# Norms and last output blocks by halves of the tokens in a two-layer hybrid encoder

## The chip, the cores and the metric

The kernel runs as one launch on one core of a Trainium2 chip. The time is device microseconds (us) of that core: the median of three runs was 3239.95 (3239.34 to 3239.95). The engines are named as in the profile: PE is TensorE, PEld its weight load, DVE is VectorE, ACT is ScalarE, POOL is GpSimd, SP is SyncE, which issues most DMAs.

## The reference

Two layers over 1024 tokens of width 1024 (float32). Cut to what matters:

```
h = x; c_act = silu(c)
for i in 0, 1:
    sh_m, sc_m, g_m, sh_f, sc_f, g_f = split(c_act @ ada_w[i] + ada_b[i])    # modulation
    hn = rms_norm(h, norm_mix[i]) * (1 + sc_m) + sh_m
    y = dsa_mixer(hn) if i == 0 else rwkv7_mixer(hn)
    h = h + g_m * y
    hn = rms_norm(h, norm_ffn[i]) * (1 + sc_f) + sh_f
    u = causal depthwise conv of width 3 over tokens (hn @ w_up[i]) + conv_b[i]
    h = h + g_f * ((silu(u[:, :2816]) * u[:, 2816:]) @ w_down[i])
return rms_norm(h, norm_final)
rms_norm(x, g) = x / sqrt(mean(x * x over the width) + 1e-6) * g
```

The first mixer scores all keys for each token with a small indexer, keeps the top 256 admissible ones, and runs 16 heads of latent attention on them. The second is an RWKV-7 recurrence. Both end in a projection by a 1024 x 1024 matrix.

## The kernel before, in words

Activations lie with the width on the 128 partitions: h is 8 tiles (KT) of 128 x 1024 tokens (S). A half (HALF) is 512 tokens, and each matmul writes 128 x 512. Every large product is made of three passes of matmuls, high by high, high by low and low by high (`passes3`, L137). The high and low parts of weights are made by POOL: SP loads a block of 128 output columns to one of two staging buffers `w_raw`, POOL writes `w_hi` by a multiplication with ones (L149) and `w_lo` by a subtraction (L151), two operations each for half a block. `stream_loop` (L155) does this for a stage. A load waits until the block two earlier is split, the split waits until the block two earlier is used.

Each engine has one instruction stream, the order of the code's parts (`k.parts`). The streams meet by semaphores, and a stage ends in a barrier of PE, ACT and DVE (`stage_end`, L125). No scheduler reorders them.

The joints between stages are all alike. An output block m of a projection or of the FFN's down product is added to h by DVE over all 1024 tokens (L767, L864, L1684: "residual"). `NormFront` (L423) then has ACT square that tile (L444) and DVE add it up (L453). After the last block, PE sums the accumulated squares over the partitions by 8 matmuls with one column (`pe_end`, L467). Then comes `norm_stage` (L472): mean on DVE (L517), root on ACT with the load of its table (L500), reciprocal on DVE (L524), 8 transposes on PE that spread it (L512), and for each tile a scaled tile (DVE, L545), its high part (ACT, L505) and its low part (DVE, L531). PE takes a tile when its low part is there.

The FFN has 22 tiles of width in 11 parts of two; the down product adds 8 output blocks of two tiles each (12 matmuls) into h in every part. Ten parts go through a loop and one, the last, follows it. Modulation vectors of later stages are made beside: DVE multiplies rows of `ada_w` by c (L620, L1676), PE sums over the partitions (L627, L1646).

In the attention, DVE searches the threshold of the top 256 keys by bits, one block of 128 queries per search: rounds (`look`, `settle`) and at the end of each search `search_end`. Nineteen rounds (`EARLY`, L1490) of the first search stand ahead of the loop over pairs of heads, the rest and other searches inside it. After the loop ACT issues loads of h (L1379, h had been spilled) and of six modulation rows (L1629), and then makes the high parts of the attention's output (`split_tiles`, L828), DVE the low parts (L833); the projection's PE waits for each.

`out_stage` (L2970) is the last: the norm without modulation writes y (L545), PE transposes it (64, L2989), ACT and DVE copy rows of 128 tokens, SP stores them.

## Time and profile before

| | us |
|---|---|
| median of three runs | 3239.95 |
| profiled execution | 3243.58 |
| its span | 3241.8 |
| PE busy in it | 2996.2 (92%) |
| DVE busy | 1661.1 (51%) |
| POOL busy | 1472.4 (45%) |
| ACT busy | 1077.8 (33%) |
| mean granted clock of TensorE | 0.957 |

The profile is of one execution, and its rows are of that one. The span runs from its first to its last instruction. Busy shares are means over stages that differ. What a joint costs is read from the timeline: the last matmul ahead of it, the first behind it, and what each of PE's waits was for. Numbers in square brackets of a row are the idle time before it and the instruction that ended it. A granted clock of 1.0 is 2.4 GHz, of 0.5 it is 1.2 GHz. Grouped rows (x8) give the time over the whole group. A matmul of float32 ones with one column has two records (16 for 8).

### The profile page before, as it was taken

What the parts mean: (1) busy time and instruction counts of PE and PEld (TensorE: products, weight loads), DVE (VectorE), ACT (ScalarE), POOL (GpSimd) and SP (SyncE); (2) the same over time, 40 slices, a digit from 0 to 9 for tenths busy, and PEclk for the clock granted to TensorE, in tenths of its full rate; (3) what the DMA queues carried; (4) which work ended last, traced back from release to release, by engine and by line L of the source; (5) the groups of instructions that cost most, each with busy time, mean ns of one, the idle gap of its engine ahead of it and who ended that gap; (6) DMA issues with size and microseconds to landing.
All of it is one profiled execution on the core that took longest, in us unless ns stands there. A gap on an engine that the chain in (4) does not pass through costs nothing.

```text
span 3241.8 us, 62740 instructions
## 1 busy us (share of the span) xinstructions
PE 2996.2 (92%) x25842; PEld 2379.9 (73%) x25842; DVE 1661.1 (51%) x2291; ACT 1077.8 (33%) x1634; POOL 1472.4 (45%) x1464
## 2 busy tenths in 40 slices
PE   5889899889999999998999798999898999999997
PEld 5734467777878877786678588888777888778886
DVE  4477887665444544457033255665545444443446
ACT  2267787222111211125332255455312211211112
POOL 1101000335666656666365355565364554555543
PEclk6889999999999999998999799999998999999998
DMA  5300000522322222221532311211211111111112
GB/s 204 119 12 14 1 2 2 204 82 74 90 83 66 73 74 84 84 59 51 191 121 80 111 49 50 89 56 51 86 49 39 46 41 42 44 55 52 40 42 73
DMA packets 229752, 225.80 MB, mean 70 GB/s; under 512 B 16398, under 2 KB 198241, under 8 KB 229537
## 3 DMA queue, kind: packets, MB, share of 16 engines
q1 hardware_dynamic: 217232, 180.42, 18.0%
q10 hardware_dynamic: 12305, 42.25, 3.6%
q8 instruction: 167, 2.74, 0.4%
q14 instruction: 48, 0.39, 0.0%
HBM read 185.15 MB, written 37.22 MB: 69 GB/s over the span
## 4 chain that ended last, share of the span: by engine, by line
PE 43%; issue 19%; POOL 18%; DVE 8%; DMA 5%; ACT 3%; POOLq 1%; SPq 0%; DVEq 0%; ACTq 0%; PEldq 0%; PEld 0%
POOL w_hi L149 9%; POOL w_lo L151 9%; PE ps L139 7%; PE ps L141 7%; PE ps L140 7%; DMA w_raw<-in_f_w_up_dram 2%; PE ps L2571 2%; DMA w_raw<-in_f_w_down_dram 2%; PE ps L2583 2%; PE ps L1187 2%; PE ps L1176 1%; PE ps L1198 1%; PE ps L2496 1%; PE ps L2620 1%; PE ps L2610 1%
## 5 line engine op out<-in xcount | busy, mean ns | idle before, releaser
L149 POOL TENSOR_TENSOR w_hi<-w_raw,ones 128x128 fp32r<-128x128 f32 (+1 forms) x568 | 471.6, 830 | 1074.1 <-PE ps L141 950.1
L751 DVE SCALAR_TENSOR_TENSOR uc<-u,pc,uc 128x1024 f32<-128x1024 f32 x176 | 272.0, 1546 | 602.2 <-ACT uc L735 589.2
L139 PE MATMUL ps<-hn_hi,w_hi 128*128 128x512 f32 x1408 | 553.2, 393 | 26.6 <-POOL w_lo L151 18.5
L151 POOL TENSOR_TENSOR w_lo<-w_raw,w_hi 128x128 fp32r<-128x128 f32 (+1 forms) x568 | 554.3, 976 | 44.5
L140 PE MATMUL ps<-hn_lo,w_hi 128*128 128x512 f32 x1408 | 550.2, 391 | 0.0
L141 PE MATMUL ps<-hn_hi,w_lo 128*128 128x512 f32 x1408 | 550.1, 391 | 0.0
L734 ACT ACTIVATE u<-ps 128x1024 f32<-128x1024 f32 x88 | 90.5, 1028 | 939.1 <-PE ps L141 934.4
L139 PEld LDWEIGHTS ps<-hn_hi,w_hi 128*128 128x128 f32 x1408 | 265.8, 189 | 90.4 <-issue 18.1
L141 PEld LDWEIGHTS ps<-hn_hi,w_lo 128*128 128x128 f32 x1408 | 265.6, 189 | 55.8
L140 PEld LDWEIGHTS ps<-hn_lo,w_hi 128*128 128x128 f32 x1408 | 265.9, 189 | 54.8
L139 PE MATMUL ps<-g_hi,w_hi 128*128 128x512 f32 x704 | 279.8, 397 | 10.7 <-POOL w_lo L151 9.7
L767 DVE SCALAR_TENSOR_TENSOR h<-ps,mod,h 128x1024 f32<-128x1024 f32 x176 | 220.4, 1281 | 123.6 <-PE ps L141 123.6
L141 PE MATMUL ps<-g_hi,w_lo 128*128 128x512 f32 x704 | 274.5, 390 | 0.0
L140 PE MATMUL ps<-g_lo,w_hi 128*128 128x512 f32 x704 | 274.4, 390 | 0.0
L139 PE MATMUL ps<-rp_x_hi,w_hi 128*128 128x512 f32 x448 | 180.6, 403 | 4.4 <-DVE rp_x_lo L531 4.4
L141 PE MATMUL ps<-rp_x_hi,w_lo 128*128 128x512 f32 x448 | 177.8, 397 | 0.0
L140 PE MATMUL ps<-rp_x_lo,w_hi 128*128 128x512 f32 x448 | 177.3, 396 | 0.0
L139 PEld LDWEIGHTS ps<-g_hi,w_hi 128*128 128x128 f32 x704 | 132.1, 188 | 61.4 <-issue 23.6
L141 PEld LDWEIGHTS ps<-g_hi,w_lo 128*128 128x128 f32 x704 | 132.1, 188 | 28.1
L140 PEld LDWEIGHTS ps<-g_lo,w_hi 128*128 128x128 f32 x704 | 132.2, 188 | 25.5
L1856 DVE SCALAR_TENSOR_TENSOR rp_x<-rp_hn,pc,rp_x 128x1024 f32<-128x1024 f32 x24 | 41.8, 1750 | 159.7 <-ACT rp_x L1831 159.7
L1807 POOL TENSOR_TENSOR w_hi<-w_raw,ones 128x512 fp32r<-128x512 f32 x48 | 59.9, 1248 | 136.1 <-PE ps L141 125.9
(380 smaller groups left out, 5652.1 us busy)
## 6 DMA issues: line engine op xcount, KB each, us to landing
w_raw<-in_f_w_up_dram SPq DMA_DIRECT2D x88, 512.0 KB, 3.9
f_ada_w<-in_ada_w_dram SPq DMA_DIRECT2D x48, 512.0 KB, 3.9
rwkv_scratch<-rp_stage ACTq DMA_DIRECT2D x48, 512.0 KB, 3.0
w_raw<-in_f_w_down_dram SPq DMA_DIRECT2D x176, 128.0 KB, 2.2
rc_raw<-rwkv_scratch SPq DMA_DIRECT2D x32, 512.0 KB, 4.0
d_r<-in_ada_w_dram ACTq DMA_DIRECT2D x24, 512.0 KB, 5.8
ada_w<-in_ada_w_dram SPq DMA_DIRECT2D x16, 512.0 KB, 8.6
xin<-in_x_dram SPq DMA_DIRECT2D x8, 512.0 KB, 7.2
```

Of the source, the lines that this page charges most:

```text
L139: pe.matmul(out, w_hi, x_hi, start=first, stop=False)
L140: pe.matmul(out, w_hi, x_lo, start=False, stop=False)
L141: return pe.matmul(out, w_lo, x_hi, start=False, stop=last)
L149: pool.tensor_tensor(hi, raw, one, ALU.mult).then_inc(k.w_hi_done, 1)
L151: pool.tensor_tensor(k.w_lo[s][:, tiles, :], raw, hi.bitcast(F32), ALU.subtract).then_inc(k.w_split if n else k.w_half, 1)
L734: act.activation(u[wi][:, 2:S + 2], k.ps[2 * s + wi][:, :], ACT.Copy).then_inc(f["u_copy"], 1)
L751: dve.scalar_tensor_tensor(out=c[wi][:, :], in0=u[wi][:, tap:tap + S], scalar=k.pc[:, bass.ds(i * (2 * FF_TILES) + col, 1)], in1=c[wi][:, ...
L767: dve.scalar_tensor_tensor(out=k.h[:, m, :], in0=k.ps[m % (3 if last else 4)][:, :], scalar=k.mod[:, gate:gate + 1], in1=k.h[:, m, :], op0 ...
L1187: last = pe.transpose(turn(c)[:, i * P:(i + 1) * P], x[A % 2][e][:, t * P:(t + 1) * P], k.ident[:, :])
L1807: pool.tensor_tensor(hi, raw, one, ALU.mult).then_inc(k.w_hi_done, 1)
L2571: last = pe.matmul(bank(4 + h)[hs(1 - c), at(x)], tg[hs(c), x, h, G_M, :], ul[hs(c), 0, h, x, :], start=True, stop=True)
L2583: u_last = pe.matmul(bank(h)[hs(c), at(x)], ul[hs(1 - c), 1, h, x, :], z[hs(1 - c), h, x, :], start=begin, stop=lv == LV[-1], skip_group_c ...
```

## The change

- **Norms by halves.** Squares, sums, mean, root, reciprocal and transposes are made for 512 tokens at a time, and each tile in two halves: 16 scaled, high and low parts of 128 x 512. The first half's numbers are made while PE still works on the second half's output blocks. The second half's last squares, its mean, reciprocal and transposes stand inside the next stage, between the half tiles. PE's first product of the next stage takes all tiles of the first half, then those of the second.
- **Projections.** The last two output blocks (6 and 7) are made half by half: (6,0), (7,0), (6,1), (7,1), with the first half's sums and transposes set in (6,1) and (7,1).
- **FFN.** The last part's 8 blocks come from two loads of 512 KB (128x2x512). POOL splits them by four pairs of 512-wide operations into what was `hn_lo`. PE waits for both and does 16 steps of 6 matmuls, the 8 blocks of half 0 first, and adds each step's half tile to h by DVE.
- **Output.** `out_stage` is gone. ACT writes h times the gain to y beside the last steps, PE transposes it unscaled by the root, rows 0 to 3 during steps 11 to 14, and the reciprocal root is a scale of the copy out of PSUM. Eight row buffers take the place of four.
- **Attention.** 22 rounds ahead of the loop, the ends of the searches 2 to 5 set earlier and, for 4 and 5, in parts. At its end the high and low parts come ahead of the loads of h and of the rows, and ahead of DVE's run of semaphore clears.
- `dynamic_dma_scratch_size` is 4096 in the program's build.

The diff, cut to its core:

```diff
+def stream_last(k, sources, his, los):
+    b0, landed0, hi0 = k.blocks, list(k.landed), k.hi_extra
+    def raw(s):
+        return k.w_raw[s][:, :, :].rearrange("p a b -> p (a b)")
+    def sp_part(sp):
+        for j, source in enumerate(sources):
+            sp.wait_ge(k.w_split, b0 + j + 1)
+            sp.dma_start(raw(j).rearrange("p (t n) -> p t n", n=HALF), source).then_inc(k.w_landed[j], 16)
+    def pool_part(pool):
+        for j in range(2):
+            pool.wait_ge(k.w_landed[j], landed0[j] + 16)
+            pool.wait_ge(k.w_used, b0)
+            for n in range(2):
+                cols = slice(n * HALF, (n + 1) * HALF)
+                pool.tensor_tensor(his[j][:, cols], raw(j)[:, cols], k.ones[:, 0:1].to_broadcast([P, HALF]), ALU.mult
+                                   ).then_inc(k.w_hi_done, 1)
+                pool.wait_ge(k.w_hi_done, (b0 + j) * 2 + (hi0 + n + 1))
+                pool.tensor_tensor(los[j][:, cols], raw(j)[:, cols], his[j][:, cols].bitcast(F32), ALU.subtract
+                                   ).then_inc(k.w_split if n else k.w_half, 1)
+    k.parts["sp"].append(sp_part)
+    k.parts["pool"].append(pool_part)
+    k.blocks += 2
...
+    def ms_dve(self, dve, h):
+        nm, at = self.k.nm, self.part(h)
+        dve.wait_ge(nm["sum"], self.summed(h))
+        dve.tensor_scalar(self.ms[:, at], self.sums[:, at], 1.0 / D, EPS, ALU.mult, ALU.add).then_inc(nm["ms"], 1)
+    def root_act(self, act, h):
+        nm, at = self.k.nm, self.part(h)
+        if h == 0:
+            act.activation(self.k.root0[:, :], self.k.ones[:, 0:1], ACT.Sqrt)
+        act.wait_ge(nm["ms"], 2 * self.n + h + 1)
+        act.activation(self.root[:, at], self.ms[:, at], ACT.Sqrt).then_inc(nm["root"], 1)
+    def rinv_dve(self, dve, h):
+        nm, at = self.k.nm, self.part(h)
+        dve.wait_ge(nm["root"], 2 * self.n + h + 1)
+        dve.reciprocal(self.rinv[:, at], self.root[:, at]).then_inc(nm["rinv"], 1)
+    def bcast_pe(self, pe, h):
+        nm = self.k.nm
+        pe.wait_ge(nm["rinv"], 2 * self.n + h + 1)
+        for tt in range(h * TT // 2, (h + 1) * TT // 2):
+            last = pe.transpose(self.bcast[:, tt * P:(tt + 1) * P], self.rinv[:, tt:tt + 1].to_broadcast([P, P]),
+                                self.k.ident[:, :])
+        last.then_inc(nm["bcast"], 1)
+class FirstFront(NormStats):
...
+    def sums_pe(self, pe, h):
+        k, nm = self.k, self.k.nm
+        last_of = max(i for i, (_, n) in enumerate(self.order) if n == h)
+        pe.wait_ge(nm["acc"], self.acc0 + self.added(last_of + 1))
+        for tt in range(h * TT // 2, (h + 1) * TT // 2):
+            last = pe.matmul(self.sums[:, tt:tt + 1], k.sq_acc[:, tt * P:(tt + 1) * P], k.ones[:, 0:1], start=True, stop=True)
+        last.then_inc(nm["sum"], 4)
+TAIL = ((KT - 2, 0), (KT - 1, 0), (KT - 2, 1), (KT - 1, 1))
+BLOCKS_ORDER = tuple((m, n) for m in range(KT - 2) for n in range(NH)) + TAIL
+HALVES_ORDER = tuple((m, n) for n in range(NH) for m in range(KT))
...
+        if not rest:
+            for h in range(2):
+                front.ms_dve(dve, h)
+            front.scale_dve(dve)
+            for h in range(2):
+                front.rinv_dve(dve, h)
+        scaled(0)
+        if between:
+            between(dve)
+        scaled(1)
+        for i in range(LAST):
+            low(i)
+            if rest and i == 2:
+                for j in range(LAST - rest, LAST):
+                    front.dve(dve, j)
+            if rest and i == 4:
+                front.ms_dve(dve, 1)
+            if rest and i == 6:
+                front.rinv_dve(dve, 1)
+            if i + 2 < LAST:
+                scaled(i + 2)
 
     def pe_part(pe):
...
+def second_half(front):
+    def norm_pe(pe, i):
+        if i == 3:
+            front.sums_pe(pe, 1)
+        if i == 6:
+            front.bcast_pe(pe, 1)
+    return norm_pe
...
-    b2 = stream_loop(k, None, [(lambda i, m=m: down_block(PARTS // 2, 0, m), FF_TILES) for m in range(KT)])
+    b2 = stream_last(k, [w_down[:, FT - FF_TILES:FT, j * HALF:(j + 1) * HALF] for j in range(2)],
+                     [hn_lo[:, j, :] for j in range(2)], [hn_lo[:, 2 + j, :] for j in range(2)])
...
+    def last_bank(q):
+        return k.ps[q % 4 // 2][:, q % 2 * HALF:(q % 2 + 1) * HALF]
+    def pe_last(pe):
+        pe.wait_ge(f["g_free"], tiles0 + FT + 1)
+        for j in range(2):
+            pe.wait_ge(k.w_split, b2 + j + 3)
+        for q, (m, n) in enumerate(HALVES_ORDER):
+            cols = slice(n * HALF, (n + 1) * HALF)
+            pe.wait_ge(f["resid"], end0 + (q // 2 + 1 if q < 4 else q + 1))
+            for kt in range(FF_TILES):
+                w = slice(kt * HALF + m % 4 * P, kt * HALF + (m % 4 + 1) * P)
+                last = passes3(pe, last_bank(q), hn_lo[:, m // 4, w], hn_lo[:, 2 + m // 4, w],
+                               g_hi[:, kt, cols], g_lo[:, kt, cols], kt == 0, kt == FF_TILES - 1)
+                if q == 0 and kt == 0:
+                    last.then_inc(k.w_used, 2)
+            last.then_inc(f["last"], 1)
+            if layer == 0 and q == 3:
+                pe_mod(pe, 5)
+            if q == 10:
+                front.sums_pe(pe, 0)
+            if layer == 0 and q == 12:
+                front.bcast_pe(pe, 0)
+            if layer and 11 <= q < 15:
+                turned(pe, q - 11, range(KT))
...
+    def pe_out(pe):
+        pe.wait_ge(f["resid"], end0 + 4 + LAST)
+        for tt in (4, 5):
+            turned(pe, tt, range(KT - 1))
+        front.sums_pe(pe, 1)
+        for tt in (4, 5):
+            turned(pe, tt, (KT - 1,))
+        for tt in (6, 7):
+            turned(pe, tt, range(KT))
...
+    def out_act(act, tt, cols=slice(0, S)):
+        act.wait_ge(o_t, tt + 1)
+        act.wait_ge(k.nm["rinv"], 2 * front.n + tt // 4 + 1)
+        act.activation(row_of(tt)[:, cols], k.ps[(2, 2, 2, 2, 2, 0, 1, 2)[tt]][:, cols], ACT.Copy,
+                       scale=front.rinv[:, tt:tt + 1]).then_inc(copied[0], 1)
...
+def tail_dve(k, dve, front, b0, gate_col, resid, tail, ready=None, between=None):
+    for i, (m, n) in enumerate(TAIL):
+        cols = slice(n * HALF, (n + 1) * HALF)
+        if n:
+            block_done(k, dve, b0 + m)
+        else:
+            dve.wait_ge(tail, i + 1)
+            if ready:
+                ready(dve, m)
+        gate = gate_col + m
+        dve.scalar_tensor_tensor(out=k.h[:, m, cols], in0=k.ps[m % 3][:, cols], scalar=k.mod[:, gate:gate + 1],
+                                 in1=k.h[:, m, cols], op0=ALU.mult, op1=ALU.add).then_inc(resid, 1)
+        if i < 3:
+            front.dve(dve, 2 * (KT - 2) + i)
+        if i == 1:
+            if between:
+                between(dve)
+            front.ms_dve(dve, 0)
+            front.rinv_dve(dve, 0)
...
-        act.wait_ge(sem["pv"], NP)
-        for m in range(KT):
-            act.dma_start(k.h[:, m, :], spill[m, :, :]).then_inc(h_back[m], 16)
...
-    EARLY = 19
+    EARLY = 22
...
-        return {13: (2,), 14: (3,), 15: (4,), 16: (5,)}.get(A, ())
+        return {10: (2,), 11: (3,)}.get(A, ())
...
-            for m, ranked in ((6, LAST - 3), (7, LAST + 6)):
-                if A == (LAST - 4 if m == 6 else LAST + 6):
+            for m, begun, ranked in ((4, 12, 13), (5, 14, 15), (6, LAST - 4, LAST - 3), (7, LAST + 6, LAST + 6)):
+                if A == begun:
                     end_above(dve, m)
                 if A == ranked:
                     end_rank(dve, m)
-                if A == ranked + 1:
+                if A == ranked + (1 if m > 5 else 0):
...
+    x_ready = split_tiles(k, "d_o", x, x_hi, x_lo)
+    k.parts["act"].append(back_act)
     k.parts["act"].append(act_first)
-    x_ready = split_tiles(k, "d_o", x, x_hi, x_lo)
     k.parts["act"].append(act_rest)
+    k.parts["dve"].append(clear_dve)
```

Three places show how the streams are changed. ACT at the attention's end, before; d_r in the DMA row are the modulation rows' buffers, d_o_hi is the high part of the attention's output:

```order
L1318 ACTIVATE d_r,d_small<-d_r,d_small 128x1024 x2
L1303 ACTIVATE d_r<-ps 128x512 x4
L1311 ACTIVATE d_lat<-ps 128x512
L1379 DMA h<-dsa_h 128x1024 x8
L1629 DMA d_r<-in_ada_w_dram 128x1024 x6
L828 ACTIVATE d_o_hi<-d_o_t 128x1024 x8
```

and after:

```order
L1622 ACTIVATE d_r,d_small<-d_r,d_small 128x1024 x2
L1607 ACTIVATE d_r<-ps 128x512 x4
L1615 ACTIVATE d_lat<-ps 128x512
L1075 ACTIVATE d_o_hi<-d_o_t 128x1024 x8
L1907 DMA h<-dsa_h 128x1024 x8
L1935 DMA d_r<-in_ada_w_dram 128x1024 x6
```

The eight high parts have moved ahead of the 14 DMA issues.

DVE at the joint before the first FFN, before: L1684 is the residual, L453 the sum of squares, L545 the scaled tile, L531 the low part:

```order
L1684 SCALAR_TENSOR_TENSOR h<-ps,mod,h 128x1024
L453 TENSOR_TENSOR d_lat<-d_lat 128x1024
L1692 TENSOR_TENSOR mod<-ps,pc 128x24
L517 TENSOR_SCALAR nm_small<-ps 128x8
L520 TENSOR_SCALAR scl<-mod 128x8
L522 TENSOR_TENSOR scl<-scl,pc 128x8
L524 RECIPROCAL nm_small<-nm_small 128x8
L545 SCALAR_TENSOR_TENSOR nm_t_0<-h,scl,ps 128x1024
L545 SCALAR_TENSOR_TENSOR nm_t_1<-h,scl,ps 128x1024
L531 SCALAR_TENSOR_TENSOR hn_lo<-nm_t_0,mod,hn_hi 128x1024
```

and after, from the fourth low part on: L633 is the scaled half tile, L639 the low part, L487 the mean and L499 the reciprocal of the second half:

```order
L639 SCALAR_TENSOR_TENSOR hn_lo<-nm_t_0,mod,hn_hi 128x512
L487 TENSOR_SCALAR nm_small<-ps 128x4
L633 SCALAR_TENSOR_TENSOR nm_t_1<-h,scl,ps 128x512
L639 SCALAR_TENSOR_TENSOR hn_lo<-nm_t_0,mod,hn_hi 128x512
L633 SCALAR_TENSOR_TENSOR nm_t_1<-h,scl,ps 128x512
L639 SCALAR_TENSOR_TENSOR hn_lo<-nm_t_1,mod,hn_hi 128x512
L499 RECIPROCAL nm_small<-nm_small 128x4
L633 SCALAR_TENSOR_TENSOR nm_t_0<-h,scl,ps 128x512
L639 SCALAR_TENSOR_TENSOR hn_lo<-nm_t_1,mod,hn_hi 128x512
```

The L633 behind the reciprocal is half tile 8, the first of the second half; the L639 behind it is the low part of half tile 7. The second half's numbers stand between the first half's tiles.

PE at the program's end, before, from the last three of 96 matmuls of the last part on: L467 are the sums of squares, L512 the transposes of the root, L2989 those of the output:

```order
L139 MATMUL ps<-g_hi,w_hi 128x512
L140 MATMUL ps<-g_lo,w_hi 128x512
L141 MATMUL ps<-g_hi,w_lo 128x512
L467 MATMUL ps<-ones,sg 128x1 x8
L512 MATMUL ps<-ident,nm_small 128x128 x8
L2989 MATMUL ps<-ident,y 128x128 x64
```

and after, the last step's six matmuls (hn_lo holds the weights' parts) and what stands about them:

```order
L875 MATMUL ps<-ident,y 128x128 x8
L143 MATMUL ps<-g_hi,hn_lo 128x512
L144 MATMUL ps<-g_lo,hn_lo 128x512
L145 MATMUL ps<-g_hi,hn_lo 128x512
L143 MATMUL ps<-g_hi,hn_lo 128x512
L144 MATMUL ps<-g_lo,hn_lo 128x512
L145 MATMUL ps<-g_hi,hn_lo 128x512
L875 MATMUL ps<-ident,y 128x128 x14
L573 MATMUL ps<-ones,sq_acc 128x1 x4
L875 MATMUL ps<-ident,y 128x128 x18
```

Transposes of the output (L875) now stand ahead of the last step, and the last sums (L573) among them; L512's are gone here.

## Rows read from the trace of the kernel before

**Rows 1.** The page's busy time, share and instructions of each engine:
```profile
PE 2996.2 (92%) x25842; PEld 2379.9 (73%) x25842; DVE 1661.1 (51%) x2291; ACT 1077.8 (33%) x1634; POOL 1472.4 (45%) x1464
```

**Rows 2.** PE's waits: line, releaser, total us, times, longest us:
```profile
PE ps L512 <- DVE nm_small L524: 15.2, 5, 5.0
PE ps L139 <- DVE hn_lo L531: 8.1, 2, 4.1
```

**Rows 3.** Timeline, projection to FFN: start, us, instruction [idle before <-releaser]:
```profile
686.29 1.84 PE L1646 MATMUL ps<-ones,d_r 128*128 128x1 f32 x16
690.18 3.01 PE L467 MATMUL ps<-ones,d_lat 128*128 128x1 f32 x16 [2.05 <-DVE d_lat L453]
695.43 1.94 PE L512 MATMUL ps<-ident,nm_small 128*128 128x128 f32 x8 [2.24 <-DVE nm_small L524]
697.41 2.47 DVE L545 SCALAR_TENSOR_TENSOR nm_t<-h,scl,ps 128x1024 f32<-128x1024 f32 x2 [2.12 <-PE ps L512]
701.44 0.77 PE L139 MATMUL ps<-hn_hi,w_hi 128*128 128x512 f32 x1 [4.07 <-DVE hn_lo L531]
```

**Rows 4.** Windows: busy us by engine, granted clock, DMA share, GB/s:
```profile
357.00:360.00 3.00, 2.75 (x16) 1.36 (x14) 2.93 (x11) 2.46 (x8) 0.00 (x0) 0.54 0.01 3
701.00:704.00 3.00, 2.56 (x6) 2.10 (x7) 2.93 (x4) 1.21 (x2) 0.00 (x0) 0.50 0.94 290
```

**Rows 5.** Timeline of PE, second projection to FFN:
```profile
2447.24 0.39 PE L141 MATMUL ps<-rc_y_hi,w_lo 128*128 128x512 f32 x1
...
2447.92 0.39 PE L141 MATMUL ps<-rc_y_hi,w_lo 128*128 128x512 f32 x1
...
2463.82 0.76 PE L139 MATMUL ps<-hn_hi,w_hi 128*128 128x512 f32 x1 [4.07 <-DVE hn_lo L531]
```

**Rows 6.** Timeline, attention output to its projection:
```profile
580.88 3.78 ACTq L1379 DMA_DIRECT2D h<-dsa_h  x8
...
588.20 7.69 ACT L828 ACTIVATE d_o_hi<-d_o_t 128x1024 fp32r<-128x1024 f32 x8 [8.46 <-issue]
...
591.22 0.77 PE L139 MATMUL ps<-d_o_hi,w_hi 128*128 128x512 f32 x1 [10.38 <-DVE d_o_lo L833]
```

**Rows 7.** Timeline of PE in the attention loop:
```profile
356.31 1.65 PE L1176 MATMUL ps<-d_k_t,d_o_t 64*128 64x384 f32 x4 [3.27 <-DVE d_small L1563]
```

**Rows 8.** Timeline of PE, setup to attention:
```profile
83.05 0.80 PE L139 MATMUL ps<-d_hn_hi,w_hi 128*128 128x512 f32 x1 [3.87 <-DVE d_hn_lo L531]
```

**Rows 9.** Timeline, end of the first FFN and next stage's start:
```profile
1435.59 0.46 POOL L151 TENSOR_TENSOR w_lo<-w_raw,w_hi 128x128 fp32r<-128x128 f32 x1
...
1439.60 1.28 DVE L767 SCALAR_TENSOR_TENSOR h<-ps,mod,h 128x1024 f32<-128x1024 f32 x1 [1.44 <-PE ps L141]
1440.81 5.48 DVE L620 SCALAR_TENSOR_TENSOR f_ada_acc<-f_ada_w,cact,f_ada_acc 128x1024 f32<-128x1024 f32 x4
...
1481.79 0.77 PE L139 MATMUL ps<-rp_x_hi,w_hi 128*128 128x512 f32 x1 [4.38 <-DVE rp_x_lo L531]
```

**Rows 10.** The page's DMA issues: count, KB each, median us to landing:
```profile
w_raw<-in_f_w_up_dram SPq DMA_DIRECT2D x88, 512.0 KB, 3.9
```

**Rows 11.** Timeline of POOL, 512-wide splits behind the second projection:
```profile
2448.46 1.04 POOL L149 TENSOR_TENSOR w_hi<-w_raw,ones 128x512 fp32r<-128x512 f32 x1 [5.08 <-PE ps L141]
2449.58 1.27 POOL L151 TENSOR_TENSOR w_lo<-w_raw,w_hi 128x512 fp32r<-128x512 f32 x1
2450.80 2.08 POOL L149 TENSOR_TENSOR w_hi<-w_raw,ones 128x512 fp32r<-128x512 f32 x1
```

**Rows 12.** Timeline, second FFN's end and the output stage:
```profile
3181.29 0.46 POOL L151 TENSOR_TENSOR w_lo<-w_raw,w_hi 128x128 fp32r<-128x128 f32 x1
...
3206.63 0.39 PE L141 MATMUL ps<-g_hi,w_lo 128*128 128x512 f32 x1
...
3218.65 10.62 DVE L545 SCALAR_TENSOR_TENSOR y<-h,pc,ps 128x512 f32<-128x512 f32 x16 [2.12 <-PE ps L512]
```

**Rows 13.** Timeline of VectorE, scoring before the attention loop:
```profile
200.18 5.03 DVE L1527 SCALAR_TENSOR_TENSOR d_dist<-d_r,d_wi,d_dist 128x512 f32<-128x512 f32 x6 [0.31 <-ACT d_r L1334]
```

532 lines of the change are left out of this document (310 added, 222 removed).

## The prediction

> **What bounds the kernel now.** I read the page's busy row first: TensorE (PE) is busy for 2996.2 of 3241.8 us [rows 1]. A change that leaves its matmuls alone can only win in the 245 us in which it waits, and in what a wait costs behind it. The waits of PE come next [rows 2]: five waits for the reciprocal of the norm's root take 15.2 us, two for the first low part of the normalised tile 8.1. They stand at a few joints between stages, so I went through these one by one in the timeline.
>
> The joint before the first FFN shows the pattern [rows 3]. The last output matmul ends near 686.45; PE's queue then issues, from 686.29, 16 sums for modulation, then 2.05 us idle, 16 sums of squares, 2.24 idle, 8 transposes that spread the reciprocal root, 4.07 idle, and the first FFN matmul at 701.44: 15.0 us, of which 6.8 is PE work. Then PE runs at half its clock: granted 0.50 from 701 to 704 (1.2 GHz of 2.4), behind an idle stretch of 4 us [rows 4]. The joint before the second FFN is the same, 2448.15 to 2463.82, 15.67 us; its rows also give PE's pace at full clock, three matmuls in 0.68 us, 0.227 each [rows 5].
>
> All sums below are made against the profiled execution (3243.58 us, span 3241.8). It is 3.6 above the median of 3239.95, so I subtract that from the result.
>
> **The change, joint by joint** (+ is time won).
>
> *Setup to attention, +2.5.* The first matmul waits at 83.05 for a chain of 8 transposes, a scaled tile, its high and its low part [rows 8], the same chain as in [rows 3] (transposes 1.94, scaled tiles 1.24 each). Halved: 0.97 off the transposes, about 0.6 off each of three operations, less the second reciprocal. From 1.5 to 3.2; I take 2.5. The table load stays, since nothing of the stage may begin before its barrier.
>
> *Attention, +3.9.* The searches of blocks 2 to 5 close during the loop. The longest close, block 5's, fills VectorE just ahead of the point where PE waits 3.27 us for the softmax sums, issuing at 356.31 [rows 7]. With three more rounds before the loop and the parts of this close set in earlier iterations, the softmax sums that PE needs come about 3.5 us earlier; 0.4 comes from the start. The three rounds before the loop run beside PE's projection work. If they aren't covered, up to 3 us are lost; if the half clock behind the wait goes too, 2 more are won. Range 0.5 to 6.
>
> *Attention output to its projection, +6.5.* Before, ScalarE issues 8 loads of h (3.78 us from 580.88) and then 6 of modulation rows, and only at 588.20 starts on the high parts; PE, idle for 10.38 us, goes on at 591.22, 3.02 behind that start [rows 6]. Now the high part comes first. The output's last piece is there 0.8 us into PE's wait, near 581.6, so PE starts near 581.6+3.02 = 584.6 and something for semaphores, instead of 591.22. What is late next: the loads of h and of the rows. They issue some 9 us later than before (behind eight activations, 7.69 us [rows 6]), h is needed only at the first residual block, near 605, and the rows' sums have the whole projection. This can give back 0 to 3; I take none, as eight blocks of 48 matmuls, 10.9 us each, lie ahead. Range 3.5 to 7.
>
> *Projection to first FFN, +4.7.* Still on PE in a row: 16 sums of modulation 1.84, 16 of squares (at full clock the same 1.84), 8 transposes about 1.0 beside other work. The gap that stays: residual half block 0.66, two scaled half tiles 1.3 (half of [rows 3]), low part 0.7, and 1.0 for the matmul's drain and semaphores: 3.7. Then two new stalls. VectorE's order puts the scaled tile 8, which waits for the second half's transposes, ahead of the low part 7, for which PE waits; PE does those transposes only after step 6. So PE stands for transposes 0.5 + scaled 0.66 + low 0.45: 1.6, and 0.4 where the second mean stands before low parts. Sum 1.84+1.84+1.0+3.7+2.0 = 10.4 against 15.0. The half clock behind the gap I leave as it was.
>
> *Second mixer's projection to second FFN, +7.2.* No modulation here: 3.7+1.84+1.0+2.0 = 8.5 against 15.67.
>
> *First FFN to second mixer, -5.0.* The 8 last down blocks read two 512 KB loads in place of eight of 128 KB. Each may be issued only when the staging buffer is free, that is when POOL has split the loop's last two blocks; the second of these ends at 1436.05 [rows 9], the first one block of PE work (12 x 0.227 = 2.7) ahead. A 512 KB load takes 3.9 us [rows 10], so the two land near 1437.4 and 1440.1. POOL then has four pairs of 512-wide operations at 1.04+1.27 us [rows 11], 9.2 us; beside VectorE's four modulation rows (1440.81, 5.48 us, [rows 9]) a pair is slower: the high part took 2.08 beside a VectorE add of two SBUF tiles [rows 11]. I add 4.4, so both splits are ready at 1451. PE ends the loop near 1439.45 (VectorE takes up its last block at 1439.60, [rows 9]) and waits for both: 11.7 us where before a 128-column block flowed on. Then 1.9 for the half clock, 21.8 for 16 steps of 6 matmuls, 1.84 modulation, 1.4 sums and transposes of the first half, a gap of 4.0, a lag of VectorE of 1.5, and 3.3 for the second half inside the next stage: 47.4. Before, the same stretch from 1439.45 to 1481.79 [rows 9] took 42.35. Bounds: without contention the stall is 7.3 and the sum -0.6; with every POOL operation at 2.1 it is 15 and the sum -8.
>
> The Trainium skill ("SBUF — State Buffer", section "SBUF: two separate sides") says that VectorE and GpSimd share a port pair which one instruction holds as a whole, for VectorE operations with two SBUF inputs. This is the rule that speaks against the moved splits: by it POOL stands still for all of the 5.48 us, so the splits end near 1452.1 and the joint costs 1 us more, 3213.8. The high part at 2.08 against 1.04 [rows 11] agrees in direction.
>
> *Second FFN to the output, +7.5.* The same starvation without modulation rows: the loop's last split ends at 3181.75 [rows 12], the one before 2.7 ahead, loads land near 3183.0 and 3185.7, splits end at 3192.3, PE starts at 3192.75. The loop ends near 3185.1 (the last matmul's end 3206.86 [rows 12] less 21.8), so 7.65 idle, plus 2 of half clock. 21.8 of matmuls, 0.9 of first sums and 3.7 for the 32 transposes of four output rows end at 3221.3. Before, the end was 3206.86, but 35 us followed: squares and sums, root, 16 scaled tiles of 10.62 us [rows 12], 64 transposes, the last copies and their stores. Now behind the last matmul stand residual 1.1, square 0.7, add 0.8, sums 1.0, root and reciprocal 1.0, transposes of the last rows beside these, last scaled row 1.0 and its store, 3.9 as a load of that size [rows 10], with its start and close 2.2 to 4.2: 11.7 to 13.7. End 3233 to 3235 against 3241.8; range 5 to 9.5.
>
> Sum 2.5+3.9+6.5+4.7+7.2-5.0+7.5 = 27.3. 3243.58-27.3 = 3216.3 profiled; less 3.6, **3212.7** as the median.
>
> **Rivals.**
> *A. TensorE keeps its clock.* The gaps before the FFNs shrink from about 4 us three times to one of 3.7. If that is short enough for the clock, 1.6 to 2.5 us are won at each of three joints (seven matmuls at 0.227 take twice as long at half the clock, 1.6 more; the joint's longer start at half clock up to 2.5): about 3207. With no contention on POOL (4.4) it would be 3202. For: before, three idle stretches stand in a row in these joints, with little work between [rows 3]; now one stands behind matmuls in full flow. Against: a wait of 3.27 [rows 7] left the clock at 0.54 in the trace [rows 4].
> *B. The halves only move the wait.* If VectorE's longer row of short operations stalls PE as long as the gap did, the joints before the two FFNs give nothing (-11.9) and 27.3 becomes 15.4: 3224.5. With h arriving late at the projection (3) and POOL at its upper bound (3) it is 3230.5. For: after a half norm VectorE has 32 half-wide operations, 21.1 us, against 21.8 us of PE work in the first two weight blocks, nearly no slack.
> *C. Slower: a half-wide VectorE operation costs far more than half.* There are six stretches (four norms, two FFN ends) in which PE needs one pair of 32 per 21.9 us. At x us each they lose 6 x (32x - 21.9), which eats the 27.3 from x = 0.83. The 128x512 tiles of the output norm took 0.664 (10.62/16, [rows 12]), against. But the six scoring operations of that size at 200.18 took 5.03, 0.84 each [rows 13], for, since each needs the one before, as a low part does: 6 x 5.0 = 30, 3242.5. At 0.95, halfway between 0.66 and the 1.24 of a full tile [rows 3], it is 51, 3264.
> The Trainium skill ("VectorE: DVE Perf Modes", section "The TRN2 errata — SBUF-src ops pay a fixed extra latency per instruction") gives a fixed part per instruction that small tiles pay again each time. Its formula makes 0.69 us of a 512-wide fp32 tensor_tensor, an estimate by that page; six stretches would then lose about 1 us, 3214. The 0.664 agrees.
>
> **How the numbers follow.** The forecast has 0.62 (its own range 3203 to 3223), A 0.15, B 0.14, C 0.04, and 0.05 that an unseen wait eats the gain to no change. The range reaches over A and most of B, 3193 to 3230. A difference of 0.2%, 6.5 us, is about what this measurement tells from none. Faster by more: the forecast, A, B and a part of the rest, 0.92; within it 0.05; slower, the upper part of C and a share of the rest, 0.03.
>
> **What the changed profile would show.** PE's wait for the attention output's low part near 3 us, not 10.38. Four transposes in a row, not eight, before each norm, and gaps of 3 to 4 us ahead of the FFNs' first matmuls. At step 7 to 8 of each norm a PE wait of 1 to 2 us on a low part. At both FFN ends one PE wait on POOL's split, about 11 us and 7.5 us: the largest new rows. A last FFN matmul later than before by 11 to 15 us less what was won ahead of it, and an end 12 to 14 us behind it. The forecast is wrong if those two waits are absent or over 15, if half-wide VectorE operations take over 0.75, or if the projection's first residual waits for h.

## The result, and the profile after

The changed kernel takes 3229.94 us (median of 15 runs, 3221.07 to 3237.85), the one before 3241.88 (15 runs, 3233.60 to 3244.66). The ratio is 0.9969, with a 95% interval of 0.9959 to 0.9978: 10.0 us faster (7.1 to 13.3; the two medians lie 11.9 apart). The forecast was 3212.7, from a base of 3239.95, so 27.3 faster. The sign was right, the size was not: about a third of it came. 3229.94 lies at the very end of the stated range (3193 to 3230). That end was drawn for other causes (rival B, h late at the projection, POOL slower still) than the one that made the time long, so that it holds is luck. The profiled execution took 3229.62 us, with a span of 3227.8 against 3241.8.

The page of the changed kernel, busy time of each engine (answers to [rows 1]):

```profile
PE 2990.6 (93%) x25834; PEld 2371.0 (73%) x25834; DVE 1684.7 (52%) x2397; ACT 1105.9 (34%) x1733; POOL 1443.5 (45%) x1416
```

Its waits of PE (line, releaser, total us, times, longest; answers to [rows 2]):

```profile
PE ps L143 <- POOL w_lo L155: 34.0, 63, 6.6
PE ps L143 <- POOL hn_lo L227: 18.1, 2, 10.9
...
PE ps L143 <- DVE hn_lo L639: 11.7, 4, 4.3
...
PE ps L143 <- POOL w_lo L2116: 5.5, 1, 5.5
...
PE ps L505 <- DVE nm_small L499: 3.6, 1, 3.6
PE ps L143 <- DVE d_o_lo L1080: 3.4, 1, 3.4
```

The first row, waits for weight splits all through the kernel, mostly short, was there before too (31.9 us in 65 waits). Of the five waits for the root's reciprocal (15.2 us) one of 3.6 is left. The new rows are two waits for POOL's last splits (10.9 and 7.1 us, forecast 11.7 and 7.65), and one of 5.5 us for a split that the forecast doesn't have at all.

Where the time went is read from the starts of PE's high by high matmuls, whose first and last start the view by line gives for each operand. Stretches in us, of the profiled executions:

| stretch | before | after | won | forecast |
|---|---|---|---|---|
| start to first attention matmul | 83.1 | 80.4 | 2.7 | 2.5 |
| from there to the projection, without PE's wait ahead of it | 497.7 | 497.0 | 0.7 | 3.9 |
| PE's wait ahead of the projection | 10.4 | 3.4 | 7.0 | 6.5 |
| projection, gap and first up blocks | 209.3 | 205.6 | 3.7 | 4.7 |
| first FFN's products to first RWKV matmul | 681.3 | 683.0 | -1.7 | -1.7 |
| RWKV projections, first to last matmul | 345.1 | 357.2 | -12.1 | -3.3 |
| recurrence (not changed) | 524.2 | 519.5 | 4.7 | 0 |
| second projection to last up block | 810.2 | 804.4 | 5.8 | 7.2 |
| last up block to last down matmul | 44.9 | 63.8 | -18.9 | -14.3 |
| from there to the end | 35.6 | 13.5 | 22.1 | 21.8 |
| sum | 3241.8 | 3227.8 | 14.0 | 27.3 |

The forecast's -5.0 for the first FFN's end is divided as it was worked out: 3.3 for the second half inside the RWKV stage, the rest ahead of it. The recurrence, which the change doesn't touch, took 514.6 to 527.8 us in the thirteen profiles of this study; its 4.7 lie inside that scatter, and without them the sum is 9.3, beside the 10.0 of the ratio. So one stretch lost 8.8 more than forecast, the output 4.3 more, and the attention didn't give its 3.2.

The joint before the first FFN, after (timeline of PE, answers to [rows 3]), and the clock behind it ([rows 4]; the third last column of a window is the granted clock):

```profile
683.17 0.64 PE L143 MATMUL ps<-hn_hi,w_hi 128*128 128x512 f32 x1 [4.34 <-DVE hn_lo L639]
...
690.30 0.95 PE L573 MATMUL ps<-ones,sq_acc 128*128 128x1 f32 x8
...
695.72 0.60 PE L505 MATMUL ps<-ident,nm_small 128*128 128x128 f32 x4
...
697.82 0.50 PE L143 MATMUL ps<-hn_hi,w_hi 128*128 128x512 f32 x1 [1.50 <-DVE hn_lo L639]
```

```profile
683.00:687.00 4.00, 3.83 (x10) 3.08 (x11) 4.00 (x6) 1.45 (x2) 1.04 (x1) 0.57 1.04 357
```

The joint is built as forecast: one gap of 4.34 in place of three, four transposes at 0.60, and a stall of 1.50 at half tile 7. The clock still falls (0.57), so the rival in which TensorE keeps its clock is out here. It is out in all nine profiles of the changed order in this study: the 4 us behind the gaps of 4.33 to 4.38 ahead of the two FFNs have a granted clock of 0.50 to 0.63, though in three of them the first matmul of the second FFN still took only 0.47 to 0.49.

The gap is 0.64 longer than the 3.7 of the forecast. Its sum has 0.7 for the first low part; that one took 1.53, beside a split of POOL (timeline of POOL and DVE), and 1.52 at the second FFN (2446.66, again beside a split):

```profile
681.32 1.05 POOL L153 TENSOR_TENSOR w_hi<-w_raw,ones 128x512 fp32r<-128x512 f32 x1
681.38 1.53 DVE L639 SCALAR_TENSOR_TENSOR hn_lo<-nm_t,mod,hn_hi 128x512 fp32r<-128x512 f32 x1
```

The RWKV stage, after (POOL and PE), where the 12.1 went:

```profile
1469.40 0.77 PE L143 MATMUL ps<-rp_x_hi,w_hi 128*128 128x512 f32 x1 [3.59 <-DVE rp_x_lo L639]
...
1485.24 0.50 PE L143 MATMUL ps<-rp_x_hi,w_hi 128*128 128x512 f32 x1 [1.50 <-DVE rp_x_lo L639]
...
1503.50 0.79 PE L143 MATMUL ps<-rp_x_hi,w_hi 128*128 128x512 f32 x1 [5.45 <-POOL w_lo L2116]
```

```profile
1493.73 1.61 POOL L2107 TENSOR_TENSOR w_mu<-w_raw,pc 128x512 f32<-128x512 f32 x1 [37.08 <-PE ps L145]
...
1502.19 1.26 POOL L2116 TENSOR_TENSOR w_lo<-w_raw,w_hi 128x512 fp32r<-128x512 f32 x1
```

The same of POOL before:

```profile
1496.13 1.49 POOL L1791 TENSOR_TENSOR w_mu<-w_raw,pc 128x512 f32<-128x512 f32 x1 [15.57 <-PE ps L141]
...
1505.03 1.29 POOL L1800 TENSOR_TENSOR w_lo<-w_raw,w_hi 128x512 fp32r<-128x512 f32 x1
```

PE starts the first block 12.4 us earlier than before, [rows 9], but POOL starts the next block's split only 2.4 earlier. POOL waits for PE to be past the first half of the weight buffers. In the order by tiles that is at tile 4 of 8, 14.3 us behind the block's first matmul (1481.79 to 1496.13). In the order by halves each weight tile is used twice, once for each half of the tokens, and the signal comes at half tile 12 of 16, 24.3 us behind it. The split takes some 10 us beside VectorE; of the block only 4.3 us are left to hide it. PE stands for 5.45 us, and its granted clock behind that is 0.57:

```profile
1505.00:1510.00 5.00, 5.00 (x15) 3.90 (x14) 0.00 (x0) 0.92 (x1) 4.92 (x5) 0.57 0.00 0
```

The attention, after: the waits of 2.28 and 3.27 ([rows 7] has the second) are gone or small (1.29 is left), and a new one of 3.67 stands ahead of them, behind the ends of searches 2 and 3. The first of the two before, and then two rows after:

```profile
346.29 1.97 PE L1209 MATMUL ps<-ident,d_small 128*64 128x128 f32 x16 [2.28 <-DVE d_small L1545]
```

```profile
322.88 1.98 PE L1513 MATMUL ps<-ident,d_small 128*64 128x128 f32 x16 [3.67 <-DVE d_small L1846]
...
348.23 1.09 PE L1513 MATMUL ps<-ident,d_small 128*64 128x128 f32 x16 [1.29 <-DVE d_small L1846]
```

The end of the first FFN, after (DVE, POOL and PE; answers to [rows 9] and [rows 11]). The first two of POOL's four pairs took 1.04 and 1.26 to 1.30 an operation. The last two, beside VectorE's four modulation rows, took twice as long, and PE waits 10.91.

```profile
1428.18 8.30 DVE L752 SCALAR_TENSOR_TENSOR f_ada_acc<-f_ada_w,cact,f_ada_acc 128x1024 f32<-128x1024 f32 x4
...
1429.20 2.02 POOL L224 TENSOR_TENSOR hn_lo<-w_raw,ones 128x512 fp32r<-128x512 f32 x1
1431.30 2.12 POOL L227 TENSOR_TENSOR hn_lo<-w_raw,hn_lo 128x512 fp32r<-128x512 f32 x1
...
1437.85 0.76 PE L143 MATMUL ps<-g_hi,hn_lo 128*128 128x512 f32 x1 [10.91 <-POOL hn_lo L227]
```

The slowing goes both ways: the same four rows took 5.48 before [rows 9] and 8.30 here, and the two pairs 8.4 (1429.20 to 1437.60) where the two ahead of them took 4.75. So POOL lost 3.7, beside the 4.4 that the forecast added and the 5.48 of the rule by which it would stand still.

The output, after (timelines of PE, ACT and DVE; [rows 12] are those of before): the wait for the splits, and then a table load of 1.28 us that stands ahead of the first half's root.

```profile
3181.64 0.76 PE L143 MATMUL ps<-g_hi,hn_lo 128*128 128x512 f32 x1 [7.14 <-POOL hn_lo L227]
...
3200.69 1.28 ACT L492 ACT_TABLE_LOAD   x1
...
3202.31 0.18 DVE L499 RECIPROCAL nm_small<-nm_small 128x4 f32<-128x4 f32 x1 [2.21 <-ACT nm_small L494]
...
3205.46 1.73 PE L875 MATMUL ps<-ident,y 128*128 128x128 f32 x8 [2.33 <-ACT out_row L895]
```

### The profile page after: what moved, and what is told of

Its sections match the earlier page's. It is cut to its first block, busy times and chain, and to the rows that moved or that the text cites. A ratio compares the mean times of both kernels' runs of the same rounds, so it can differ in the third digit from the quotient of the medians.

```text
span 3227.8 us, 62888 instructions
## 1 busy us (share of the span) xinstructions
PE 2990.6 (93%) x25834; PEld 2371.0 (73%) x25834; DVE 1684.7 (52%) x2397; ACT 1105.9 (34%) x1733; POOL 1443.5 (45%) x1416
## 3 DMA queue, kind: packets, MB, share of 16 engines
q1 hardware_dynamic: 213968, 180.42, 18.1%
## 4 chain that ended last, share of the span: by engine, by line
PE 37%; issue 19%; POOL 19%; DVE 6%; DMA 5%; ACT 3%; POOLq 1%; SPq 0%; DVEq 0%; ACTq 0%
POOL w_hi L153 9%; POOL w_lo L155 9%; PE ps L143 7%; PE ps L144 7%; PE ps L145 7%; DMA w_raw<-in_f_w_up_dram 2%; PE ps L2889 2%; DMA w_raw<-in_f_w_down_dram 2%; PE ps L2901 2%; PE ps L1491 1%; PE ps L1480 1%; PE ps L1502 1%; PE ps L2814 1%; PE ps L2938 1%; PE ps L2928 1%
## 5 line engine op out<-in xcount | busy, mean ns | idle before, releaser
L153 POOL TENSOR_TENSOR w_hi<-w_raw,ones 128x128 fp32r<-128x128 f32 (+1 forms) x536 | 442.6, 826 | 1059.9 <-PE ps L145 933.9
L155 POOL TENSOR_TENSOR w_lo<-w_raw,w_hi 128x128 fp32r<-128x128 f32 (+1 forms) x536 | 535.1, 998 | 42.0
L144 PEld LDWEIGHTS ps<-hn_lo,w_hi 128*128 128x128 f32 x1408 | 266.0, 189 | 54.2
L143 PE MATMUL ps<-g_hi,w_hi 128*128 128x512 f32 x640 | 254.9, 398 | 10.2 <-POOL w_lo L155 9.3
L967 DVE SCALAR_TENSOR_TENSOR h<-ps,mod,h 128x1024 f32<-128x1024 f32 x160 | 200.0, 1281 | 114.9 <-PE ps L145 114.9
L145 PE MATMUL ps<-g_hi,w_lo 128*128 128x512 f32 x640 | 249.7, 390 | 0.0
L144 PE MATMUL ps<-g_lo,w_hi 128*128 128x512 f32 x640 | 249.2, 389 | 0.0
L143 PEld LDWEIGHTS ps<-g_hi,w_hi 128*128 128x128 f32 x640 | 120.0, 188 | 57.7 <-issue 22.9
L145 PEld LDWEIGHTS ps<-g_hi,w_lo 128*128 128x128 f32 x640 | 120.1, 188 | 25.8
L144 PEld LDWEIGHTS ps<-g_lo,w_hi 128*128 128x128 f32 x640 | 120.2, 188 | 23.1
```

The costliest lines, as they stand in the source:

```text
L143: pe.matmul(out, w_hi, x_hi, start=first, stop=False)
L144: pe.matmul(out, w_hi, x_lo, start=False, stop=False)
L145: return pe.matmul(out, w_lo, x_hi, start=False, stop=last)
L153: pool.tensor_tensor(hi, raw, one, ALU.mult).then_inc(k.w_hi_done, 1)
L155: pool.tensor_tensor(k.w_lo[s][:, tiles, :], raw, hi.bitcast(F32), ALU.subtract).then_inc(k.w_split if n else k.w_half, 1)
L967: dve.scalar_tensor_tensor(out=k.h[:, m, :], in0=k.ps[m % 4][:, :], scalar=k.mod[:, gate:gate + 1], in1=k.h[:, m, :], op0=ALU.mult, op1=AL ...
```

## The experiments

My theory was that three things ate the gain: the late release of weights in the RWKV stage, waits for both splits at the FFNs' ends, and a table load at the output, while the new search only moved a wait. The rival was that the half-wide operations cost more than half, and that the waits for POOL only stand where PE would otherwise wait for VectorE. Single runs of one kernel scatter by over 0.5% (3230.95 to 3249.58 for the kernel before in the last group), so each experiment is read twice: by its ratio to before, and by the stretch that it changes.

**The late release alone, in the kernel before.**

```diff
-                    if kt == KT // 2 and s == 0 and n == 0:
+                    if kt == (KT // 2 if j else 6) and s == 0 and n == 0:
                         last.then_inc(sem["half"], 1)
```

> The kernel before, in which the first low-rank block of the RWKV projection tells POOL that the first half of the weight buffers is free at its tile 6 of 8 instead of tile 4 (one signal moved, nothing else). Theory (the late release of the weights costs what the halves lost in this stage): POOL starts its next split near 1501.6 instead of 1496.13, needs 10.2 us, and PE, done with the block near 1505.7, waits 5 to 6 us for it and then runs some matmuls at half clock: 6 to 8.5 us slower than before (3248 to 3250 on a base of 3241.9), with one wait of PE on POOL's L1800 of about 6 us. Rival (the 12 us lost there come from the half-wide operations of VectorE and ScalarE, and POOL's lateness would be absorbed by later blocks): within 2 us of before.

Measured: 3236.43, ratio 1.0005 (0.9995 to 1.0015). The ratio tells it neither from no change nor from the 3.9 us that the stretch shows: the RWKV projections took 349.0 us instead of 345.1 (345.0 and 345.3 in the two other profiles of the kernel before with this signal as it was). The wait is there, but only 2.43 long (timelines of PE and POOL):

```profile
1511.39 0.49 PE L139 MATMUL ps<-rp_x_hi,w_hi 128*128 128x512 f32 x1 [2.43 <-POOL w_lo L1800]
```

```profile
1504.36 1.04 POOL L1791 TENSOR_TENSOR w_mu<-w_raw,pc 128x512 f32<-128x512 f32 x1 [21.23 <-PE ps L141]
...
1510.08 1.26 POOL L1800 TENSOR_TENSOR w_lo<-w_raw,w_hi 128x512 fp32r<-128x512 f32 x1
```

POOL was released 20.0 us behind the block's start, and its six operations took 7.0 us, not the 10.2 of before, as VectorE's last operations on two tiles had just ended (1504.39). The mechanism is shown by the stretch and by the wait, at about half of the 6 to 8.5 expected: later blocks did not absorb it. The median doesn't show it; taken alone it fits the rival as well.

**POOL's two free operations ahead of the wait, in the changed kernel.**

```diff
+        pool.tensor_tensor(cur, cur, prev, ALU.subtract).then_inc(k.w_hi_done, 1)
+        freed(pool, j, n)
         pool.tensor_tensor(hi[1], prev, one, ALU.mult).then_inc(k.w_hi_done, 1)
-        pool.tensor_tensor(cur, cur, prev, ALU.subtract).then_inc(k.w_hi_done, 1)
...
-                freed(pool, j, n)
                 scaled_pool(pool, j, n)
```

> The changed kernel, in which POOL makes the first two of its six operations per half block (product with mu, raw less product), which touch no weight buffer PE reads, ahead of its wait for the release instead of behind it. Theory: PE's wait of 5.45 us before the second low-rank block falls by the 2.9 us of these two operations, to about 2.5, and the half clock behind it shrinks: 3 to 5 us faster than the changed kernel (3225 to 3227, ratio to before near 0.9955). Rival: PE's wait goes to the low parts of VectorE or to another split, and the time stays at 3229.9.

Measured: 3220.89, ratio 0.9954 (0.9938 to 0.9969) against 0.9969 of the changed kernel; the two intervals overlap, so the stretch and the wait carry this. The stretch went from 357.2 to 350.0. PE's wait fell from 5.45 to 0.70, and the matmul behind it is at full clock (0.49, not 0.79):

```profile
1470.25 0.47 PE L143 MATMUL ps<-rp_x_hi,w_hi 128*128 128x512 f32 x1 [3.50 <-DVE rp_x_lo L639]
...
1484.97 0.50 PE L143 MATMUL ps<-rp_x_hi,w_hi 128*128 128x512 f32 x1 [1.50 <-DVE rp_x_lo L639]
...
1498.48 0.49 PE L143 MATMUL ps<-rp_x_hi,w_hi 128*128 128x512 f32 x1 [0.70 <-POOL w_lo L2117]
```

This is the main evidence. The stretch is 7.2 shorter, but not all of it is POOL's. PE's first matmuls here ran faster by chance (0.47, not 0.77, with the same code and work ahead), and PE came to the second half's sums 1.1 us sooner, ahead of any wait for POOL. So about 6 of the stretch's 12.1 us hang on when POOL may write, more than the 3 to 5 expected. The other profiles say the same: 354.5 to 357.2 us in five with the late release, 349.5 to 350.7 in four with this edit. Of the 4.9 us still lost against before, the forecast had the second half's sums and transposes and the stall at half tile 7 (3.3 in all). The remaining 1.6 are nearly all POOL again, in later waits of this profile that are not there before (view of waits; 0.7, 0.2 and 0.5):

```profile
PE ps L143 <- POOL w_lo L2117: 0.9, 2, 0.7
PE ps L143 <- POOL w_lo L2126: 0.5, 1, 0.5
```

**PE starts on the first split.**

```diff
-        for j in range(2):
-            pe.wait_ge(k.w_split, b2 + j + 3)
+        pe.wait_ge(k.w_split, b2 + 3)
         for q, (m, n) in enumerate(HALVES_ORDER):
+            if q == 4:
+                pe.wait_ge(k.w_split, b2 + 4)
```

> The changed kernel, in which PE starts the last down steps of both FFNs when the first 512 KB is split, and waits for the second only ahead of step 4. Theory (PE starves because it waits for both): the waits of 10.9 and 7.1 us fall by two pairs of POOL operations, 4.2 and 4.7 us, so 8 to 9 us faster than the changed kernel, or up to 11 with less half clock: 3219 to 3222, ratio near 0.993. Rival (the output rows' and VectorE's chain sets the end of the second FFN, and the RWKV projection waits for POOL anyway): only 0 to 4 us.

Measured: 3211.90, ratio 0.9925 (0.9910 to 0.9940), 14 us below the changed kernel by the ratios. The first FFN's stretch fell from 683.0 to 677.5, the second's end from 63.8 to 57.2: 12.1 us. PE's wait is 2.36 at the first and 2.34 at the second:

```profile
3174.64 0.47 PE L143 MATMUL ps<-g_hi,hn_lo 128*128 128x512 f32 x1 [2.34 <-issue]
```

It starts at full clock (0.47 against 0.76). The starvation is real and as large as forecast, and three quarters of it (18.1 us of waits, 4.7 left) come from one wait that asks for more than the first four steps read.

**The old search in the changed kernel, and the new one in the kernel before.** The diff of the first is that of the change undone, of the second that part of it alone. Both diffs have three smaller edits beside these (where ScalarE stands for the rounds ahead of the loop, and the parts of the ends 4 and 5):

```diff
-    EARLY = 19
+    EARLY = 22
...
-        return {13: (2,), 14: (3,), 15: (4,), 16: (5,)}.get(A, ())
+        return {10: (2,), 11: (3,)}.get(A, ())
...
```

> The changed kernel with the attention's search as it was before (19 rounds ahead of the loop, the four ends in iterations 13 to 16). Forecast: this part was worth 3.9, so it would be 3.9 slower, 3233.8. Theory from the changed trace: the part only moved the wait (3.67 us at 322.9 in place of 2.28 and 3.27 at 346 and 356) and is worth 1 to 2 at the start and nothing in the loop: 0 to 1.5 slower, 3230 to 3231.5; PE's waits of 2.28 and 3.27 come back and the one at 322.9 goes.

> The kernel before with the changed attention search alone (22 rounds ahead of the loop, the ends of searches 2 to 5 earlier). Forecast: 3.9 faster. Theory (the wait is only moved): PE's loop from its first scores to its last values stays at 310 to 311 us, with a wait of about 3.7 us near iteration 12 in place of 2.28 and 3.27 later; within 1 us of before, not to be told from it by the median.

Measured: the first 3227.02, ratio 0.9967 (0.9955 to 0.9978), so nothing; the second 3244.69, ratio 1.0012 (0.9999 to 1.0025), nothing or slightly slower. Old search in the changed kernel, then new search in the kernel before (timeline of PE):

```profile
339.62 1.98 PE L1513 MATMUL ps<-ident,d_small 128*64 128x128 f32 x16 [2.27 <-DVE d_small L1846]
...
349.64 1.65 PE L1480 MATMUL ps<-d_k_t,d_o_t 64*128 64x384 f32 x4 [3.35 <-DVE d_small L1864]
```

```profile
331.07 1.97 PE L1209 MATMUL ps<-ident,d_small 128*64 128x128 f32 x16 [3.67 <-DVE d_small L1545]
```

From the first scores to the last values PE took 310.70 us in the changed kernel and 310.69 with the old search; before it was 310.1, and with the new search alone 312.2. The waits have changed places and not their sum: 5.6 us before, and 5.0 for the two rows shown after. I read this as the same VectorE work standing ahead of other softmax sums; no run takes that apart further. The attention's term of 3.9 was wrong.

The profile of the changed kernel with the old search is 3.0 us shorter ahead of the loop. 1.7 of these lie in 16 matmuls that stand before the search begins: they took 7.13 us at a granted clock of 1.00, 8.83 at 0.81 in the changed kernel and 9.78 at 0.72 in a third profile. The rest may be the search. From the first attention matmul to the projection, without the wait ahead of it, the new search alone took 501.9 in the kernel before, and three profiles with the old one 495.7 to 498.8; in the changed kernel it is 496.7 to 499.1 with the new search (seven profiles) and 493.9 and 496.7 with the old one. So the moved search is likelier to cost 1 to 4 us than to gain, but the ratios don't settle it.

**The attention's high and low parts first, in the kernel before.**

```diff
-    k.parts["act"].append(act_first)
     x_ready = split_tiles(k, "d_o", x, x_hi, x_lo)
+    k.parts["act"].append(back_act)
+    k.parts["act"].append(act_first)
+    k.parts["dve"].append(clear_dve)
```

> The kernel before, with one part of the change alone: the high and low parts of the attention's output ahead of ScalarE's 14 loads and of VectorE's semaphore clears. Theory: this part is worth what its wait says, 10.4 us falling to 3.4, so 7 us faster than before (ratio 0.9978), the projection's span of 94.4 us unchanged or 1 to 2 shorter by less half clock. Rival (the loads, issued later, come late for the first residual blocks or for the modulation rows): part of it is given back inside the projection, 0 to 4 us in all.

Measured: 3231.33, ratio 0.9980 (0.9967 to 0.9992). The wait fell to 3.42, and the projection took 94.1 us against 94.4, so nothing is given back there. From the projection to the FFN's first down block it took 2.0 longer (211.3 against 209.3), but so did the kernel before with only the search changed (211.2); PE's waits are the same, and the granted clock in the 10 us behind the gap is 0.70, not 0.84. The wait's row:

```profile
582.84 0.76 PE L139 MATMUL ps<-d_o_hi,w_hi 128*128 128x512 f32 x1 [3.42 <-DVE d_o_lo L833]
```

This part alone is 6.5 us by the ratio (2.6 to 10.7), and by the wait 7.0: about two thirds of what the whole change gained.

**Low part 7 ahead of scaled half tile 8.**

```diff
+            if rest and i == 7:
+                scaled(KT)
-            if i + 2 < LAST:
+            if i + 2 < LAST and not (rest and i == 6):
                 scaled(i + 2)
```

> The changed kernel, in which VectorE makes the low part of half tile 7 ahead of the scaled half tile 8 (which waits for the second half's transposes), in the three norms that stand at a joint. Theory (PE's stall there comes from this order): the waits of 1.50 us at half tile 7 fall to about 0.8 at half tile 8, 0.7 us each, 2 us in all; the RWKV one gives nothing while POOL is late. Rival (the second half's transposes themselves set it): the wait is 1.5 again, on half tile 8, and the time that of the changed kernel.

Measured: 3227.70, ratio 0.9974 (0.9962 to 0.9987), not to be told from the changed kernel. In the trace the stall is one half tile later and 0.99 long:

```profile
700.26 0.50 PE L143 MATMUL ps<-hn_hi,w_hi 128*128 128x512 f32 x1 [0.99 <-DVE hn_lo L639]
```

The order is a third of that stall. For the rest VectorE waits 1.36 for the transposes that PE makes behind its step 6. The effect, 0.5 at each joint, is below what a median shows.

**The root's table early.**

```diff
     def act_last(act):
+        act.activation(k.root0[:, :], k.ones[:, 0:1], ACT.Sqrt)
```

(and not in the first `root_act` there.)

> The changed kernel, in which ScalarE loads the root's table ahead of the last 16 down steps of each FFN instead of at step 11. Theory (at the output, the load of 1.28 us stands ahead of the first half's root, so the first output rows and, through them, PE's transposes are late: PE waits 2.33 us for the copied row): from the last FFN matmul group to the end 1.3 to 2.5 us less, and nothing elsewhere: 0.04 to 0.08%. Rival (the row's copy waits for ScalarE's squares and gains, not for the table): under 0.5 us.

Measured: 3225.34, ratio 0.9959 (0.9944 to 0.9974), by itself not to be told from the changed kernel's 0.9969. From the last up block to the last down matmul it took 60.7 us instead of 63.8 (63.4 to 63.8 in four profiles that leave these steps as they were), 3.1 less, and PE's waits for copied rows fell from 4.0 to 2.3 us. The view of waits, changed kernel and then this one:

```profile
PE ps L875 <- ACT out_row L895: 4.0, 3, 2.3
```

```profile
PE ps L875 <- ACT out_row L895: 2.3, 3, 0.9
```

The load is 1.28 us long but cost 3.1. The first reciprocal stands on VectorE ahead of the residual of step 11, so the table delays the residuals and squares too, and with them the row copies that PE waits for: 1.7 of the 3.1. The other 1.4 is clock. Behind the wait of 2.33 the changed kernel ran 4 us at 0.57, and the next step's six matmuls took 2.5 us instead of 1.5; here the longest such wait is 0.87, and the clock stays at 1.00. These are its windows, 3205.4 to 3209.4 in the changed kernel and 3209 to 3213 here:

```profile
3205.40:3209.40 4.00, 3.94 (x15) 3.38 (x16) 1.28 (x1) 1.14 (x3) 0.00 (x0) 0.57 0.33 134
```

```profile
3209.00:3213.00 4.00, 4.00 (x23) 2.91 (x21) 2.63 (x3) 1.88 (x4) 0.00 (x0) 1.00 0.64 258
```

**All four edits, then with a still earlier start, then with the old search.**

> The changed kernel with all four edits: POOL's two free operations ahead of its wait, PE starting on the first split, low part 7 first, table early. Theory: the single effects add up, 7 (RWKV projection) + 12 (both FFN ends) + 1.5 + 1.5 = 22 us faster than the changed kernel, ratio to before 0.990, near 3209 on a base of 3241.9. Rival (they overlap: an earlier start of the RWKV stage meets POOL or the loads again, and an earlier second FFN end meets the output rows): 14 to 18.

> The kernel with all four edits, in which the first of the last down steps starts on the first half of the first split (one pair of POOL operations earlier) and waits for the second only ahead of its second tile. Theory: PE's first three matmuls go 1.2 to 2.3 us earlier but the next three wait for the pair, so 0.7 us per FFN at most, and a shorter idle stretch: 0 to 1.5 us faster than all four edits (ratio 0.989). Rival: POOL's second pair sets it, no change.

> The kernel with all four edits and the attention's search as before. Theory (the search's change is worth nothing): 3203 to 3205 on the base of 3238 to 3242, ratio 0.989, as with the new search; PE's loop 310 to 311 us. Rival (the change of the search does cost, as the 3 us between two profiles of the changed kernel suggest): 2 to 3 us faster, ratio 0.988.

The earlier start is this:

```diff
-        pe.wait_ge(k.w_split, b2 + 3)
+        pe.wait_ge(k.w_half, b2 + 1)
...
+                if q == 0 and kt == 1:
+                    pe.wait_ge(k.w_split, b2 + 3)
```

Measured: 3203.65, ratio 0.9890 (0.9873 to 0.9907) with the four edits; 3208.79, 0.9894 (0.9876 to 0.9913) with the earlier start; 3210.84, 0.9901 (0.9882 to 0.9919) with the four edits and the old search. The three are one within the intervals. The stretches show nothing of the earlier start either: 678.7 at the first FFN against 677.3 with the four edits, and at the second 53.5 against 55.8, where the run with the old search has 54.2 without it. The four edits bring 35.7 us against before (30.1 to 41.2), 26 more than the change. The stretches show 21.4 of it (5.7 and 8.0 at the FFN ends, 7.7 in the RWKV projections), about the sum of the single effects. The waits of PE with the four edits, from the first FFN's end into the RWKV stage, 1415 to 1530:

```profile
PE ps L143 <- DVE rp_x_lo L639: 4.6, 2, 3.5
PE ps L143 <- issue: 2.5, 1, 2.5
PE ps L761 <- DVE f_ada_acc L754: 1.5, 1, 1.5
PE ps L573 <- DVE sq_acc L566: 1.5, 1, 1.5
PE ps L143 <- POOL w_lo L2121: 0.9, 2, 0.7
PE ps L143 <- POOL w_lo L2130: 0.5, 1, 0.5
```

## Why the prediction was right in sign and wrong in size

- **Setup joint, 2.5:** 2.7. Right.
- **Attention output to its projection, 6.5:** 7.0 by the wait, and 6.5 alone in the kernel before. Right; no cost of the late loads shows. The wait's row answers to [rows 6].
- **Joints before the two FFNs, 4.7 and 7.2:** 3.7 and 5.8. The gap, the sums and the stalls were there as worked out: gap 4.34 for 3.7, stall 1.50 for 1.6. The term that was mis-sized is the 0.7 for the first low part in the gap: it took 1.53 beside POOL's split. The rest of the two shortfalls, 0.4 and 0.8, was not taken apart.
- **FFN ends, stalls of 11.7 and 7.65:** 10.9 and 7.1. The mechanism and the size were right. VectorE's rows did slow POOL (2.02 and 2.12 an operation in this trace, 1.04 and 1.26 to 1.30 without them).
- **"3.3 for the second half inside the next stage": this step failed.** It was 12.1. The forecast counted what PE executes there, but not what PE releases there. The order by halves keeps every weight tile until the second half of the tokens has used it, so the release of the weights' first half moved from 14.3 to 24.3 us behind the block's start, and POOL's split no longer fits. The forecast put this wait at nothing. About 6 us of the 8.8 that are missing hung on it, as the experiment with the two free operations shows, about 1.4 more are POOL's later waits that this experiment leaves, and about 1 is clock at the block's start, in which the profiles differ.
- **Attention, 3.9:** 0.7 in the stretch and no gain by either experiment, rather a small cost. This step failed too. "The softmax sums that PE needs come about 3.5 us earlier" followed one wait only. It held for that one, but the moved work makes earlier sums late, with a wait of 3.67.
- **Output, 7.5:** 3.2. The tail of 11.7 to 13.7 was right (13.5). What was missed is inside the last steps: 3.1 for a table load that I priced at nothing there, nearly half of it through the clock behind the wait. The other 1.2 was not taken apart; PE's waits for copied rows were still 2.3 without the table.
- **The rivals.** A (the clock is kept): no at the FFNs' joints, 0.57 behind the gap. Its "about 4 us three times" was a misreading: [rows 3] has 2.05, 2.24 and 4.07. At the RWKV stage it came true in one profile of nine (see the last section). B (the halves only move the wait): in part and elsewhere; it happened at the RWKV stage, through POOL and not through VectorE's row. C (half-wide operations cost more than half): no. They are 0.74 to 0.75 long in the median and start 0.66 apart; only the few beside POOL's splits took 1.1 to 1.5. The formula of the Trainium skill ("VectorE: DVE Perf Modes", section "The TRN2 errata — SBUF-src ops pay a fixed extra latency per instruction") gives 0.69 for an fp32 tensor_tensor of this width, an estimate by that page; the trace's spacing agrees within 0.03, and its durations are 0.05 to 0.06 longer.
- **The signs of being wrong.** None of the three that the prediction names came: both waits on POOL are in bounds, the half-wide operations have medians of 0.74 to 0.75, and no residual waited for h. They watched the terms that were in the sum, and the failure was a wait that was not.

The sum: 27.3, less 8.8 (RWKV stage), 4.3 (output), 3.2 (attention), 1.4 and 1.0 (joints), with 0.7 more at the first two, gives 9.3, and the ratio says 10.0.

What stays open: 1.2 us at the output, 1.2 in the joints before the two FFNs, and whether the moved search costs anything. That the four edits bring 4 us more by the ratio than by their stretches is within the intervals.

## What to carry to other kernels

When a loop is turned round so that each operand is used in two passes, ask first who waits for that operand's buffer: its release moves from the middle of the block to its end, and whoever fills it loses that cover. When PE waits for several pieces at once, look at which piece the first step reads. Together they cost about 18 us here (6 and 12), more than the 12.2 that the change won at the joints of the norms (2.7, 3.7 and 5.8).

## What the runs showed of the hardware

- The clock behind an idle stretch isn't a function of its length alone. In the changed kernel PE's first RWKV matmul took 0.77 behind 3.59 us idle, in another profile 0.47 behind 3.50, with the same work ahead of both. Behind 3.50 or 3.51 idle the first 4 us there had a granted clock of 1.00 in one profile, 0.60 to 0.69 in five and 0.50 in two. Ahead of the attention's loop the same 16 matmuls took 7.13 to 10.08 us.
- POOL's 512-wide operations took 1.9 to 2.3 us beside VectorE's operations on two SBUF tiles and 1.04 to 1.3 without. VectorE pays as well: four 1024-wide rows took 8.30 instead of 5.48, and a 512-wide low part 1.53 instead of 0.75. A split that is released later, when VectorE has stopped, can so take 7.0 us and not 10.2, and give back a part of its lateness.
- The medians of one kernel moved by 7 us between groups of runs (3236.48, 3238.04 and 3243.34 for the kernel before, each group on another chip), so a kernel is compared only with its own group. The recurrence alone, which is the same code in all of them, took 514.6 to 527.8 us.
